# Latent queries and keys turned by the product itself, and the split of X2 in rooms of its own, in a two-block layer kernel

## The reference, cut to what matters

```python
def project_groups(t, w_in, q_norm, kv_norm, w_q_up, w_kv_up):
    p = jnp.einsum('bsd,de->bse', t, w_in)
    qa, ka, va, cq, ckv, kr = jnp.split(p, SPLIT_POINTS, axis=-1)
    ...
    qb = jnp.einsum('bsr,re->bse', rmsnorm(cq, q_norm), w_q_up).reshape(bt, n, H_B, NOPE_B + ROPE_B)
    kvb = jnp.einsum('bsr,re->bse', rmsnorm(ckv, kv_norm), w_kv_up).reshape(bt, n, H_B, NOPE_B + V_B)

def mla_attend(qn, qr, kn, kr, v):
    s = (jnp.einsum('bqhd,bkhd->bhqk', qn, kn, preferred_element_type=jnp.float32)
         + jnp.einsum('bqhr,bkr->bhqk', qr, kr, preferred_element_type=jnp.float32)) * MLA_SCALE
    p = jax.nn.softmax(s, axis=-1)
    o = jnp.einsum('bhqk,bkhd->bqhd', p.astype(v.dtype), v)
```

## Time and profile before

| | us |
|---|---|
| median of three runs | 642.66 (641.88 to 642.78) |
| the profiled execution | 643.4 |
| its span | 641.6 |
| TensorE busy in the span | 571.4 (89%) |
| VectorE, ScalarE, GpSimd busy | 298.9, 218.9, 40.1 |
| mean granted clock of TensorE | 0.98 |
| read from memory | 191.21 MB |

### The profile page before, as it was taken

How to read it: one execution, slowest core, us unless ns; L and a number is a source line. 1 busy time by engine, 2 the same in 40 slices (tenths; PEclk the granted TensorE clock), 3 DMA queues, 4 the chain that set the end, 5 groups by cost and what they waited for, 6 DMA issues and landing times.

```text
span 641.6 us, 8810 instructions
## 1 busy us (share of the span) xinstructions
PE 571.4 (89%) x3486; PEld 372.9 (58%) x3486; DVE 298.9 (47%) x703; ACT 218.9 (34%) x474; POOL 40.1 (6%) x73
## 2 busy tenths in 40 slices
PE   7999999999999999989999999999989755765675
PEld 6898877777867887848855454445353411311232
DVE  3355477775668977575737867125220100010002
ACT  4344444554524523484426765022110100010002
POOL 2000000000000000110002444000000000000000
PEclk9999999999999999989999999999999997898899
DMA  8594975659689883845569333668999999999994
GB/s 352 165 404 151 383 307 194 246 222 387 264 324 431 309 313 131 295 152 207 199 263 354 138 100 127 231 257 329 387 432 426 425 432 427 424 423 429 427 419 170
DMA packets 22925, 193.36 MB, mean 301 GB/s; under 512 B 4194, under 2 KB 5602, under 8 KB 11236
## 3 DMA queue, kind: packets, MB, share of 16 engines
q1 hardware_dynamic: 19140, 189.28, 74.1%
q10 hardware_dynamic: 3456, 1.94, 1.1%
q0 software_dynamic: 288, 1.57, 0.6%
HBM read 191.21 MB, written 1.06 MB: 300 GB/s over the span
## 4 chain that ended last, share of the span: by engine, by line
PE 65%; DMA 22%; DVE 5%; ACT 3%; issue 2%; SPq 2%; ACTq 0%; POOL 0%; POOLq 0%; DVEq 0%
PE bank L1255 26%; DMA ring<-in_stream 21%; PE bank L1232 6%; PE bank L1243 6%; PE bank L1877 6%; PE bank L1813 2%; PE bank L1294 2%; PE bank L1741 2%; SPq L832 2%; PE bank L1676 2%; PE bank L1643 2%; PE bank L1799 2%; PE bank L1538 2%; PE bank L1923 1%; DMA vvc<-vvc 1%
## 5 line engine op out<-in xcount | busy, mean ns | idle before, releaser
L1255 PE MATMUL bank<-weight_parts,u_parts 128*128 128x512 f32 (+2 forms) x416 | 125.8, 385 | 0.8 <-ACT mo L858 0.3
L2188 DVE TENSOR_TENSOR weight_parts<-ring,weight_parts 128x1024 fp32r<-128x1024 f32 (+2 forms) x64 | 73.2, 1179 | 36.7 <-ACT weight_parts L858 34.8
L1255 PEld LDWEIGHTS bank<-weight_parts,u_parts 128*128 128x128 f32 x416 | 76.1, 189 | 17.3 <-issue 2.0
L858 ACT ACTIVATE weight_parts<-ring 128x1024 fp32r<-128x1024 f32 (+2 forms) x64 | 63.9, 1021 | 34.0 <-PE bank L1255 21.4
L1255 PE MATMUL bank<-weight_parts,x_parts 128*128 128x512 f32 (+1 forms) x128 | 48.4, 378 | 0.0
L1255 PE MATMUL bank<-u_parts,weight_parts 128*128 128x256 f32 x192 | 36.8, 287 | 1.0 <-DVE weight_parts L2188 0.6
L1199 POOL TENSOR_TENSOR small<-small 128x1 f32<-128x1 f32 (+1 forms) x14 | 8.3, 596 | 420.4 <-DVE small L2608 200.4
L922 ACT ACTIVATE sp<-sp,small 128x128 f32<-128x128 f32 (+1 forms) x48 | 21.3, 444 | 32.9 <-DVE small L2098 32.9
L1255 PEld LDWEIGHTS bank<-u_parts,weight_parts 128*128 128x128 f32 x192 | 30.5, 191 | 2.7 <-issue 1.3
L1147 ACT ACTIVATE sp<-bank 128x512 f32<-128x512 f32 x4 | 2.4, 597 | 75.0 <-PE bank L1877 75.0
L1255 PE MATMUL bank<-x_parts,weight_parts 128*128 128x256 f32 x96 | 27.1, 283 | 0.0
...
## 6 DMA issues: line engine op xcount, KB each, us to landing
ring<-in_stream SPq DMA_DIRECT2D x38, 2048.0 KB, 9.2
parts<-in_stream SPq DMA_DIRECT2D x9, 2048.0 KB, 20.9
qk<-in_stream SPq DMA_DIRECT2D x8, 2048.0 KB, 11.7
tabs<-in_stream SPq DMA_DIRECT2D x5, 2048.0 KB, 25.4
mo<-in_stream SPq DMA_DIRECT2D x5, 2048.0 KB, 28.6
vvc<-in_stream SPq DMA_DIRECT2D x5, 2048.0 KB, 31.8
...
```

Of the source, the lines that this page charges most:

```text
L858: ins = act.activation(dst, src, ACT.Copy, scale=scale)
L1255: ins = pe_.matmul(o, lhs(a, c, i), rhs(b, c, i), start=(c == 0 and n == 0), stop=(c == chunks - 1 and n == 2))
L2188: dve.tensor_tensor(quarter(weight_parts[:, SLOT:], name, q), quarter(slot(name), name, q), quarter(weight_parts, name, q).bitcast(F32), A ...
```

## The change

The rows of `w_q_up` and `w_kv_up` are laid out anew on the host: the plain columns of all heads first, then the rotated ones (or values). `qu00`, `qu10`, `xkv00`, `xkv10`, `ckv00`, `ckv10` become products with the weight as the stationary side (`turned_pairs`), so that each leaves four heads with the head columns in rows: `qnT`, `knT`. `qu01`, `qu11` hold the rotated query columns with tokens in rows; they are rotated there (`qrow`) and turned by four turns (`qr`); four turns of the rotated key, written four times side by side (`krow`), are `kr`. The other 48 turns and their moves are gone, and `pick`, which nothing read, with them. A unit's score is a product over 64 rows plus one over 32; two heads stand side by side in the array's rows, and a step's two units are now two heads of one query tile.

X2 goes to room 4 (`qk`), ahead of KU0 in the stream; its four quarters are split behind `clT`, the high part to room 1 of `ring`, the low part in place. X0, which uses room 1, is issued after `xa12`. `hT01` on ScalarE sums the squares of tile 1 ahead of its copy, and VectorE takes mean and scaling inside `hT00` instead of behind `hT01`. `modT1` moves from ahead of `mT11` to behind `ckv11`; the load of the window mask moves to `xa01`. The order of `DENSE` and the first steps of attention are rewritten. The diff, cut:

```diff
 STREAM = (["W0", "W1", "W2", "W3", "W4", "M0", "WC", "W5", "M1", "W6", "M2", "W7", "M3", "W8", "M4", "W9", "M5",
-           "WA", "M6", "W10", "M7", "W11", "WB", "C0", "WO0", "C1", "WO1", "KU0",
-           "X2", "X1", "X0", "QU", "KU1", "OUT0", "OUT1"]
+           "WA", "M6", "W10", "M7", "W11", "WB", "C0", "WO0", "C1", "WO1", "X2", "KU0",
+           "X1", "X0", "QU", "KU1", "OUT0", "OUT1"]
...
-LATE = {"C0": 1, "WO0": 4, "C1": 0, "WO1": 1, "KU0": 0, "X2": 1, "X1": 0, "X0": 1, "QU": 0, "KU1": 1, "OUT0": 2, "OUT1": 3}
+LATE = {"C0": 1, "WO0": 4, "C1": 0, "WO1": 1, "KU0": 0, "X2": 4, "X1": 0, "X0": 1, "QU": 0, "KU1": 1, "OUT0": 2, "OUT1": 3}
...
-SPLIT_AFTER = {"hT01": "X2", "ckv11": "X2", "hT10": "X2", "hT11": "X2"}
...
-         "modT1", "mT11", "wo00", "cc0", "cc1", "wo10", "clT", "wo01", "wo11", "ckv00", "ckv01",
-         "ckv10", "hT00", "hT01", "ckv11", "hT10", "hT11",
-         "kc0", "kc1", "kc3", "xa02", "kc2", "xa12", "xa01", "xa11", "xa00", "lq0",
-         "xa10", "lq1", "lk0", "lk1", "qu00", "qu01", "lgb", "xkv00", "xkv01", "qwT0", "qu10", "qwT1", "kwT",
-         "qu11", "xkv10", "xkv11", "qm0", "qm1", "qm2", "qm3", "kx0", "kx1", "kx2", "kx3"]
+         "mT11", "wo00", "cc0", "cc1", "wo10", "clT", "wo01", "wo11", "ckv00", "ckv10",
+         "hT00", "hT01", "ckv01", "ckv11", "modT1", "hT10", "hT11",
+         "xa02", "xa12", "xa01", "xa11", "xa00", "lq0",
+         "xa10", "lq1", "lk0", "lk1", "kr", "qu01", "qu00", "lgb", "qu11", "qu10", "xkv00", "qwT0", "xkv10", "qwT1",
+         "kwT", "xkv01", "qr", "xkv11"]
...
-SPLIT_AT = {"WO0": {"wb01": (2, 0), "mT01": (0, 1), "mT11": (0, 1)}, "WO1": {"wo10": (3, 1)}}
+SPLIT_AT = {"WO0": {"wb01": (2, 0), "mT01": (0, 1), "mT11": (0, 1)}, "WO1": {"wo10": (3, 1)}, "X2": {"clT": (0, 4)}}
...
-        if name in SPLIT_AFTER:
-            k = SPLIT.index(SPLIT_AFTER[name])
-            out.append(("split", (k, sum(i == ("split", (k, q)) for i in out for q in range(4)))))
-        if name == "qu11":
+        if name == "kwT":
             out += [("pair", 0), ("mask", 0), ("mask", 1), ("soften", 0), ("soften", 1)]
         if name == "xkv11":
-            out += [("pair", 1), ("scale", 0), ("mask", 2), ("scale", 1)]
-        if name == "qm1":
-            out += [("mask", 3), ("soften", 2)]
-        if name == "kx3":
-            out += [("soften", 3), ("scale", 2)]
+            out += [("pair", 1), ("scale", 0), ("mask", 2), ("scale", 1), ("mask", 3), ("soften", 2), ("soften", 3),
+                    ("scale", 2)]
...
+        x2_parts = [parts_at("x2_high", "ring", SLOT, SLOT), parts_at("x2_low", "qk", 0, SLOT)]
...
-        kcat = view(qk, 0, 3072, "p (t h d) -> p t h d", t=2 * TOK, h=HB)
-        qcat = view(qk, 3072, 1536, "p (t h d) -> p t h d", t=TOK, h=HB)
+        krow = view(qk, SLOT, 512, "p (t h d) -> p t h d", t=2 * TOK, h=4)
+        qrow = view(qk, SLOT + 512, 512, "p (t h d) -> p t h d", t=TOK, h=HB)
...
-        qmT = turned[:, :].rearrange("p (h s) -> p h s", h=HB)
-        kmT = tabs[:, :].rearrange("p (h s) -> p h s", h=HB)
+        qnT = view(turned, 0, 1024, "p (j s) -> p j s", j=4)
+        qrT = view(turned, 1024, 512, "p (g s) -> p g s", g=2)
+        knT = view(tabs, 0, 2048, "p (j s) -> p j s", j=4)
+        krT = view(tabs, 2048, 512)
...
+            return u // 4 % 4, u % 2, u // 2 % 2
...
-                filled(eng, "kx2")
-                filled(eng, "kx3")
+                filled(eng, "qr")
+                filled(eng, "xkv11")
...
+                    if name == "X0":
+                        filled(eng, LAST_USE["X2"])
...
-                    if n:
-                        quarter_released(eng, n - 1, q)
-                    copy(quarter(weight_parts, name, q), quarter(slot(name), name, q)).then_inc(split_a, 1)
+                    if name == "X2":
+                        eng.wait_ge(split_v, 4 * SPLIT.index("WO1") + 4)
+                    elif n:
+                        quarter_released(eng, SPLIT.index("WO1") if name == "X1" else n - 1, q)
+                    high = x2_parts[0] if name == "X2" else weight_parts
+                    copy(quarter(high, name, q), quarter(slot(name), name, q)).then_inc(split_a, 1)
...
                     elif name in ("hT01", "hT11"):
-                        if name == "hT11":
-
-                            kept(eng, "modT1")
-                            eng.wait_ge(gate_row_out, 32)
-                            eng.wait_ge(vec_used, N_VEC)
-                            eng.dma_start(modr[:, 0:1024], A["window_mask"]).then_inc(wmask_in, 16)
                         turned_mod(name, hfull, mc[:, 0, 0:8], scl[:, 0, :])
-                        kept(eng, name)
                         t = int(name[2])
-                        copy(uhigh[:, 4:8, t * P:(t + 1) * P], hfull[:, 4:8, t * P:(t + 1) * P]).then_inc(high_ready, 1)
                         if t == 0:
                             eng.wait_ge(x1_ready, 2)
                             sum_squares(xn[:, 1, :], 9, sp[:, 0:D])
+                        kept(eng, name)
+                        copy(uhigh[:, 4:8, t * P:(t + 1) * P], hfull[:, 4:8, t * P:(t + 1) * P]).then_inc(high_ready, 1)
...
                         w = 512 if h < 2 else 416
+                        if name == "xa01":
+
+                            kept(eng, "modT1")
+                            eng.wait_ge(gate_row_out, 32)
+                            eng.wait_ge(vec_used, N_VEC)
+                            eng.dma_start(modr[:, 0:1024], A["window_mask"]).then_inc(wmask_in, 16)
...
+                        if h == 0:
+                            copy(qnT[:, 2 * t:2 * t + 2, :], D_(name)[:, :].rearrange("p (j s) -> p j s", j=2), name)
+                        else:
+                            copy(qrow[:, t, :, :], D_(name)[:, 0:HB * ROPE].rearrange("p (h d) -> p h d", h=HB), name)
...
+                        x = int(name[0] == "x")
+                        if h == 0:
+                            copy(knT[:, 2 * t:2 * t + 2, S * x:S * x + S], D_(name)[:, :].rearrange("p (j s) -> p j s", j=2), name)
+                        else:
+                            copy(vm[:, TOK * x + t, :, :], D_(name)[:, :].rearrange("p (h d) -> p h d", h=HB), name)
...
+            def turned_pairs(name, w, i, src, chunks):
+
+                for k in range(2):
+                    a = P * (2 * i + k)
+                    ins = product(D_(name)[:, S * k:S * k + S], lambda c: w[:, c, a:a + P], lambda c: src[:, c, :], chunks)
+                return ins
...
+                    if name == "xkv00":
+                        for i in range(TOK):
+                            kept(eng, f"lk{i}")
...
+                    if name == "qu01":
                         arrived(eng, "QU")
+                        for i in range(TOK):
+                            kept(eng, f"lq{i}")
+                    begin(name)
+                    w = weights("QU", 3, 768)
                     if h == 0:
-                        kept(eng, f"lq{t}")
+                        done(turned_pairs(name, w, t, lqT, 3), name)
+                    else:
+                        done(rows_product(name, w, 512, HB * ROPE, t, lqT, 0, 3), name)
...
+                    for g in range(2):
+                        for t in range(TOK):
+                            ins = turn(D_(name)[:, g * S + t * P:g * S + (t + 1) * P],
+                                       qrow[:, t, 4 * g:4 * g + 4, :].rearrange("p h d -> p (h d)"))
+                    done(ins, name)
...
+                    for t in range(2 * TOK):
+                        ins = turn(D_(name)[:, t * P:(t + 1) * P], krow[:, t, :, :].rearrange("p h d -> p (h d)"))
...
-                for u in (2 * s, 2 * s + 1):
-                    h, q = (u - 16) // 2, u % 2
-                    pe_.matmul(score_bank(u)[:, :], qmT[0:QK, h, q * P:(q + 1) * P], kmT[0:QK, h, :], start=True, stop=True)\
-                       .then_inc(u_scores, 1)
+                j, _, q = unit_of(2 * s)
+                cols = slice(q * P, (q + 1) * P)
+                for b in range(2):
+                    h = slice(HD * b, HD * b + HD)
+                    pe_.matmul(score_bank(2 * s + b)[:, :], qnT[h, j, cols], knT[h, j, :], start=True, stop=False,
+                               tile_position=(HD * b, 0))
+                for b in range(2):
+                    a = HD * b + ROPE * (j % 2)
+                    h = slice(a, a + ROPE)
+                    pe_.matmul(score_bank(2 * s + b)[:, :], qrT[h, j // 2, cols], krT[h, :], start=False, stop=True,
+                               tile_position=(a, 0)).then_inc(u_scores, 1)
...
-                        kept(eng, f"kx{p}")
+                        if p == 0:
+                            kept(eng, "kr")
+                        else:
+                            eng.wait_ge(mod_kept, 2)
...
+            def mean_begun(k, w, width, n_squares):
 
                 eng.wait_ge(squares, n_squares)
```

(15 more changed lines are left out.)

99 lines of the change are left out of this document (30 added, 69 removed), and 2 rows, old and new, of the table LAST_USE.

## The result

The changed kernel takes 639.15 us (median of eight runs, 637.48 to 640.41) against 642.05 us (640.86 to 643.74) for the kernel before on the same chip: a ratio of 0.994, with a 95% interval of 0.9923 to 0.9958, which is 3.85 us less (2.7 to 4.9). The two medians by themselves are 2.9 us apart, inside that interval. The profiled execution took 637.48 us with a span of 635.7, the quickest of its eight. The measured time lies 1.25 us above the forecast of 637.9 us and inside its range (636.4 to 639.4); the gain of 4.8 us was put 1 us too high by the ratio, 1.9 by the medians.

The account below looks back on a forecast made before the run. A TensorE-bound front was taken to set when the transfer-bound back starts; 5.2 (place 1) + 1.6 (place 2) - 2.0 (latent scores) = 4.8 us less, giving a median of 637.9 us, range 636.4 to 639.4.

Parts of the forecast that it names:

- What bounds it: Whole kernel: TensorE-bound front, transfer-bound back; a microsecond gained ahead of the last releases moves the end by one microsecond.
- Place 1: 273 to 298 us, around the second tile's norm, key turns and `xa02`: `xa01` starts 5.2 us sooner.
- X0, nothing: X0's load, issued only after `xa12` is filled: lands after 7.8 us and costs nothing, 0.6 us kept for the range.
- the window mask's load, nothing: The wait for the window mask's table, moved to `xa01`: over long before, its 0.5 MB wanted 40 us later.
- Place 2: 322 to 351 us, latent products, turns and first window rounds: 3.0 gained, net 1.6 us sooner, bounds 0.8 and 2.6.
- The latent scores: Eight latent steps on TensorE, 64-row plus 32-row products at 0.27 us a record: 2.0 us later.
- The estimate by the rule: Latent scores, with the skill's drain on a change of tiling mode: 0.35 us a step, 2.8 us in all.
- the 0.6 without it: Latent scores, lower bound: two pairs take 1.99 us against 1.91 for an old step, 0.6 us in all.
- (a): Rival: new waits bite (X0, X2's split, short groups, clock); gain 2.5 us, 640.2 us; chance 0.18.
- (c): Rival: transfers ahead of 506 us fill their time, so the back starts no sooner; 642.7 us; chance 0.07.
- (d): Rival: 64-row and 32-row products of the eight latent steps all run serially; 8.5 us slower, 651.2 us; chance 0.07.

Follow-up runs that it names:

- no_rope: Changed kernel without the 32-row products of the latent scores, so rotated columns do not enter; 633.08 us.
- turns_back: Changed kernel with twelve 128 x 96 turns put back between `hT11` and `xa02`; 643.28 us, the execution already 3.58 us behind before the edit.
- x2_late: Changed kernel with X2's four quarters split where the kernel before split them, still in rooms of their own; 642.84 us.
- pair_later: Changed kernel with the first window pair behind `xkv01` instead of right behind `kwT`; 636.67 us.
- scale_first: Changed kernel with VectorE scaling unit u - 2 ahead of the masking and maximum of unit u in the window steps; 636.93 us.
- rope_64: Changed kernel with the second product of each latent score over 64 rows instead of 32, wrong rows entering; 638.46 us.
- zero_rows: Changed kernel with the second latent product over 64 rows, the rotated key written twice with other heads' rows zero, result right; 637.26 us.
- one_by_one: Changed kernel with each head's two latent score products behind each other before the other head's; 687.24 us.
- squares_late: Changed kernel with tile 1's squares back behind ScalarE's copy, and mean and scaling behind VectorE's low parts; 639.64 us.

## Why the prediction was right

The sum was 5.2 + 1.6 - 2.0 = 4.8 us; measured, net of the offset, it is 5.3 - 0.3 + 0.8 - 1.9 = 3.9. That 639.15 us still lies in the range of 636.4 to 639.4 is in part luck: the forecast started from a median of three runs, 642.66 us, and from the median of eight, 642.05, the same sum and width would have given 637.3 and an upper end of 638.8.

- **What bounds it.** Right. The release moved by 3.85 us net and the end with it; `no_rope` and the table show that the back follows one for one. The medians, 2.9 us apart, cannot be told from that.
- **Place 1, 5.2: measured 5.34.** `hT10` came 1.83 sooner (1.85 in the sum), with a wait under 1.5 us and the granted clock at 1.00, `xa02` and `xa12` took 9.15 (9.2). X2's split lies in ScalarE's and VectorE's gaps without a delay. The working took the old turns at their measured duration, which is right for the sum, and it held 1.7 us of it to hang on the clock. That size holds: `turns_back` gives 1.2 us ahead of `xa02`, and the first three matmuls of `xa02` took 1.10 us before (287.59 to 288.69) in place of 0.57. The rest of the 1.37 us gained between `xa02` and `xa01` are the four turns (0.6) and the wait behind them (0.26). What the working left out is that these parts are not free of each other: with X2's split in its old place, VectorE's last low part would have held TensorE up whatever the clock and the turns did (`x2_late`).
- **X0, nothing: right; the window mask's load, nothing: measured 0.3.** X0 took 7.6 us (7.8 in the sum) and ScalarE had it in time. But `xa00` waits 0.41 us at its start for VectorE's low part, and what made that late is the load of the mask, of which the prediction weighed only the wait and the arrival: its issue of 0.34 us stands ahead of ScalarE's copy of `xa01`, on the path.
- **Place 2, 1.6: measured 0.8.** This is the mis-sized term. Behind the second pair the sum had 3.0 and 2.97 came. Ahead of it 1.4 were to be lost, and 1.85 were: the wait for `kwT` is 1.05 and not 0.8, since what happens around a copy of 0.69 us counts as well, and the short groups wait twice 0.25, not 0.3 together. Then came what I had named and taken nothing off for: the mask of unit 3 stands ahead of the scaling of unit 2 on VectorE, the masks of units 4 and 5 begin 0.27 us later for it, and the turn behind them waits 1.07 us, 0.26 more than in the kernel before. From the scores at 340.64 to the first latent step 0.35 are lost in all. `pair_later` gets the 1.05 us back and so shows the first cause. `scale_first` shows that the order on VectorE costs 1.0 us, but most of that the kernel before had too; that 0.26 of the 0.35 come by the late mask is read from the two timelines.
- **The latent scores, 2.0 later: measured 1.9.** Right in size. I took the window's 0.27 us a record for both forms; it is 0.28 for both. Counted from start to start, so that nothing is counted twice, a step's scores take 2.12 us (358.94 to 361.06) in place of 1.82 (365.16 to 366.98), in some steps 1.89: 16.9 against 14.75 in eight steps, 2.2 us. The rest of the steps is 0.3 us shorter, so two small misses cancel in part:

```profile
365.16 1.88 PE L1643 MATMUL bank<-tabs,tz 96*128 96x512 f32 x4
366.98 1.08 PE L1676 MATMUL bank<-mo 128*64 128x256 f32 x8
```

```profile
361.06 1.08 PE L1683 MATMUL bank<-mo 128*64 128x256 f32 x8
```

  The Trainium skill (TensorEngine Tiling (Array Packing), Tiling Modes) says that changing the mode, and not just the tile, drains the engine. The runs fit this and give it a size: a pair of 64-row products behind another takes 0.96 us, next to a 32-row pair 1.06, 0.2 us a step, and `rope_64` and `zero_rows` gain 1.59 us in eight steps. So most of the cost of 1.9 goes with the 32-row form; 0.3 is left for the split of the product. That it is the change of tiling, and not the 32 rows as such, is argued from the 64-row pair, which is 0.10 us dearer too when a 32-row pair stands behind it; no run has two 32-row pairs behind each other. The estimate by the rule, 2.8, was nearer than the 0.6 without it, and 2.0 was nearest.
- **The rivals.** (a) happened in part: the clock stayed and X0 was in time, but the mask's issue and the short waits took 1 us. (c) is refuted. (d) did not occur; `one_by_one` shows that its price was too low.

What stays open: what moving the mask's issue would give back, and why the clock falls in `x2_late` after waits of 1.01 and 1.14 us and not in `squares_late` after 2.56, and why it falls in `one_by_one`.
